# Attention with stacked rounded parts, values by tokens, two items a slot, and projections between the slots

## The reference

```
h  = norm0(x)*(1+scale)+shift
q,kc,vc,ks,vs,kw,vw,gl,z = h @ w_in           # NSA mixer
o  = g0*softmax(q k_cmp)v_cmp + g1*softmax(q ks)vs + g2*softmax(q kw)vw
x += gate_row0 * ((o * silu(z)) @ w_out)
# MoBA mixer: one causal softmax a head, 256 keys, the same form
x += gate_row1 * ((softmax(q k)v * silu(z)) @ w_out)
x += ffn1(norm(x)); x += mix(norm(x)) ; x += ffn2(norm(x))
```

## Time and profile before

| | us |
|---|---|
| median of 3 runs | 1009.32 (1008.92 to 1018.35) |
| the profiled execution, own time | 1017.86 |
| its span | 1016.0 |
| PE busy | 941.6 (93%) |
| DVE, ACT, POOL busy | 601.0, 515.5, 173.2 |

### The profile page before, as it was taken

One profiled execution on the slowest core, in us unless ns is written; L12 is line 12 of the kernel. 1 busy time (PEld: TensorE's weight loads), 2 busy tenths in 40 slices (PEclk: granted clock), 3 DMA queues, 4 the chain that ended last, 5 costly groups with the idle time before them and its releaser, 6 DMA issues.

```text
span 1016.0 us, 13211 instructions
## 1 busy us (share of the span) xinstructions
PE 941.6 (93%) x4823; PEld 763.2 (75%) x4823; DVE 601.0 (59%) x1192; ACT 515.5 (51%) x940; POOL 173.2 (17%) x190
## 2 busy tenths in 40 slices
PE   2689988998989988999999998999899899999997
PEld 2578976555568964788888887889788788888886
DVE  4873567766457577675555444659345765555542
ACT  2233556765434476564444443667555464444431
POOL 0015424652002651010000000426000200000000
PEclk9889999767699998999999999999999999999999
DMA  9855725444055453356555653645233555565651
GB/s 344 307 153 179 248 75 178 144 145 125 0 166 165 147 172 98 107 175 201 181 181 177 208 171 110 197 145 157 77 120 105 166 166 186 185 201 174 201 152 41
DMA packets 45391, 163.28 MB, mean 161 GB/s; under 512 B 5136, under 2 KB 5392, under 8 KB 45328
## 3 DMA queue, kind: packets, MB, share of 16 engines
q1 hardware_dynamic: 45328, 162.44, 50.0%
HBM read 161.37 MB, written 1.05 MB: 160 GB/s over the span
## 4 chain that ended last, share of the span: by engine, by line
PE 85%; DVE 8%; ACT 3%; issue 2%; DMA 1%; SPq 0%; POOL 0%; DVEq 0%; ACTq 0%
PE bank L451 55%; PE bank L460 11%; PE bank L475 5%; PE bank L610 3%; PE bank L589 2%; PE bank L588 2%; PE bank L504 2%; PE bank L547 1%; PE bank L612 1%; DVE w_lo L1313 1%; DVE ada_acc L1408 1%; PE bank L609 1%; DMA w_raw<-in_weights 1%; DVE stats L1494 1%; ACT soft L1007 1%
## 5 line engine op out<-in xcount | busy, mean ns | idle before, releaser
L888 ACT ACTIVATE w_hi<-w_raw 128x1024 fp32r<-128x1024 f32 (+2 forms) x249 | 259.2, 1047 | 203.0 <-PE bank L451 174.5
L1313 DVE TENSOR_TENSOR w_lo<-w_raw,w_hi 128x1024 fp32r<-128x1024 f32 (+2 forms) x249 | 300.8, 1224 | 101.3 <-ACT w_hi L888 101.3
L451 PE MATMUL bank<-w_hi,h_hi 128*128 128x512 f32 (+1 forms) x576 | 229.4, 398 | 15.6 <-DVE w_lo L1313 8.2
L451 PE MATMUL bank<-w_hi,h_lo 128*128 128x512 f32 (+1 forms) x576 | 225.4, 391 | 0.0
L451 PE MATMUL bank<-w_lo,h_hi 128*128 128x512 f32 (+1 forms) x576 | 224.9, 390 | 0.0
L451 PEld LDWEIGHTS bank<-w_hi,h_hi 128*128 128x128 f32 x576 | 109.5, 190 | 37.4 <-issue 16.5
L451 PEld LDWEIGHTS bank<-w_hi,h_lo 128*128 128x128 f32 x576 | 109.2, 190 | 22.9
L451 PEld LDWEIGHTS bank<-w_lo,h_hi 128*128 128x128 f32 x576 | 109.7, 190 | 20.9
L1952 POOL TENSOR_TENSOR ada_acc<-ada_acc,w_raw 128x512 f32<-128x512 f32 x56 | 73.4, 1311 | 84.0 <-ACT w_raw L892 79.4
L460 PE MATMUL bank<-h_hi,w_hi 128*128 128x256 f32 x264 | 77.9, 295 | 0.2 <-ACT tok_k L892 0.2
L460 PE MATMUL bank<-h_lo,w_hi 128*128 128x256 f32 x264 | 75.2, 285 | 0.0
(11 more groups left out here) (258 smaller groups left out, 1412.6 us busy)
## 6 DMA issues: line engine op xcount, KB each, us to landing
w_raw<-in_weights SPq DMA_DIRECT2D x298, 512.0 KB, 4.0
w_raw<-in_weights SPq DMA_DIRECT2D x4, 360.0 KB, 3.1
x<-in_x SPq DMA_DIRECT2D x1, 1024.0 KB, 7.0
gate_bias<-in_gate_bias SPq DMA_DIRECT2D x2, 512.0 KB, 9.4
out<-x SPq DMA_DIRECT2D x1, 1024.0 KB, 4.0
w_raw<-in_weights SPq DMA_DIRECT2D x3, 256.0 KB, 2.7
const<-in_constants SPq DMA_DIRECT2D x1, 413.5 KB, 7.7
cols<-in_columns SPq DMA_DIRECT2D x1, 208.5 KB, 2.5
```

Of the source, the lines that this page charges most:

```text
L451: mm = e.matmul(pb[t][:, 0:n], xs[q], ws[p], start=(k + kk == 0 and i == 0), stop=(k + kk == kts - 1 and i == 2))
L888: e.activation(w_hi[i % NSPLIT][:, 0:c], raw[v % NRAW][:, 0:c], ACT.Copy).then_inc(*rounded(v))
L1313: e.tensor_tensor(w_lo[i % NSPLIT][:, 0:c], raw[v % NRAW][:, 0:c], w_hi[i % NSPLIT][:, 0:c].bitcast(F32), ALU.subtract).then_inc(*rested(v))
```

## The change: what it does

- The two attentions are written anew (`pair_attention` on each engine). A slot is one head with both branches in NSA (16 slots) and two heads in MoBA (8). Queries are kept as `qs`, rounded part and rest stacked on 128 partitions; keys as `kh` and `kl`, each twice over the partitions. A score is two fp32r matmuls with K = 128 (kh, then kl), for both branches in one. Values are made by tokens: the turned probability is stationary, 65 columns move (64 of v and a column of ones that gives the sums). Compressed values go to the same bank (banks[7]). `evict` on DVE forms the factors (1/sum, gate) and multiplies 3 x 64 columns for both token tiles, adds the three, and stores by tokens; PE turns each closed pair of heads.
- The units of z1 come in iterations 0 to 3 of the NSA loop and six of out's eight in iterations 8 to 18, two after it. In MoBA z1 comes at 0 to 2 and five of out's eight at 6 to 10. The unit order follows.
- Ada chunks 4 and 5 of layer 0 (8 units, the gate row) are fetched among the units of q0, cmp0, q1 and cmp1, one after each two.
- Queries and keys are copied out in parts of 64 partitions: 8 copies of q (4 before), 8 of k of twice the width, and DVE subtracts the rests.
- The norm ahead of the mix turns x plainly, half of it inside the last feed-forward projection, half behind mix_lat's first unit. 1/rms is multiplied in later, at each use: eight DVE products of 512 for the gates, one more matmul of 256 columns, scales in copies for the rest.
- The bias of the gate row is loaded into gate_row itself. The output is stored in four DMAs of 256 KB.

The diff, cut to what matters:

```diff
+    z1, a, b, gate = one("nsa_z1"), ada(1, 0, 4), ada(1, 4, 6), ada(0, 4, 6)
+    heads = one("nsa_q0") + one("cmp_w1_0", CJ, 256, False) + one("nsa_q1") + one("cmp_w1_1", CJ, 256, False)
+    heads = [u for i in range(8) for u in heads[2 * i:2 * i + 2] + gate[i:i + 1]]
+    pair = lambda o, j: [o[j], o[4 + j]]
+    nsa = (in_turn(z1, a[:4]) + a[4:7] + pair(nsa_out, 0) + a[7:11] + pair(nsa_out, 1) + a[11:15]
+           + pair(nsa_out, 2) + a[15:] + pair(nsa_out, 3))
+    moba = (in_turn(b[:3], z[Z_FIRST:]) + b[3:5] + pair(moba_out, 0) + b[5:7] + pair(moba_out, 1) + b[7:]
+            + moba_out[2:4] + moba_out[6:8])
...
-             + kcvc[2:] + kskw[2:] + one("nsa_q0") + one("cmp_w1_0", CJ, 256, False)
-             + one("nsa_q1") + one("cmp_w1_1", CJ, 256, False) + one("nsa_gate", KT, P)
-             + one("nsa_vsvw") + one("nsa_z0") + in_turn(ada(0, 4, 6) + ada(1, 0, 4), one("nsa_z1"))
-             + two("nsa_out")
-             + two("moba_q") + one("moba_kv") + z[:Z_FIRST] + in_turn(ada(1, 4, 6), z[Z_FIRST:]) + two("moba_out")
+             + kcvc[2:] + kskw[2:] + heads + one("nsa_gate", KT, P)
+             + one("nsa_vsvw") + one("nsa_z0") + nsa
+             + two("moba_q") + one("moba_kv") + z[:Z_FIRST] + moba
...
+                def values(j):
+                    sl, x, p = slots[j // 2], j % 2, prob_t[j % 2]
+                    o = [ov[:, t, x + parts_ - 2, 0:HD + 1] for t in range(TT)]
+                    w.wait_ge(*p_copied.at((s, j)))
+                    for at in v_ready:
+                        w.wait_ge(*at)
+                    if x == 0:
+                        w.wait_ge(*(o_evicted.at((s, j // 2 - 1)) if j else bank_free[3]))
+                    e.matmul(o[0], p[:, 0:P], sl["values"][x][0], start=True, stop=True)
+                    e.matmul(o[1], p[:, P:2 * P], sl["values"][x][0], start=True, stop=False)
+                    mm = e.matmul(o[1], p[:, 2 * P:3 * P], sl["values"][x][1], start=False, stop=True)
+                    if x == 1 and sl["compressed"]:
+                        g, r = sl["compressed"]
+                        for t in range(TT):
+                            mm = e.matmul(ov[:, t, 0, 0:HD], pc_t[:, r, t * P:(t + 1) * P], vc[:, g, :], start=True,
+                                          stop=True)
+                    mm.then_inc(*valued((s, j)))
...
+                    if i < n:
+                        for t in range(TT):
+                            w.wait_ge(*(masked.at((s, i - 1, t)) if i else bank_free[t]))
+                            for o, q, ks in slots[i]["scores"][t]:
+                                for m, k in enumerate(ks):
+                                    mm = e.matmul(o, q, k, start=m == 0, stop=m == 1)
+                            mm.then_inc(*scored((s, i, t)))
+                    pr = slots[i - 4]["close"] if i >= 4 else None
+                    if pr is not None:
+                        w.wait_ge(*(o_summed if s == "nsa" else o_evicted).at((s, i - 4)))
+                        w.wait_ge(*p_copied.at((s, min(2 * (i - 3) + 1, 2 * n - 1))))
+                        turn(banks[6], [(tt * P, otok[:, tt, pr * P:(pr + 1) * P])
+                                        for tt in range(TT)]).then_inc(*o_turned((s, pr)))
+                        turned = pr
+                    if 0 <= i - 3 < n:
+                        values(2 * (i - 3) + 1)
+                    for x in range(2 if 0 <= i - 2 < n else 0):
+                        j = 2 * (i - 2) + x
+                        w.wait_ge(*exped.at((s, j, 1)))
+                        w.wait_ge(*(p_copied.at((s, j - 1)) if j else bank_free[2]))
...
+                        m = soft6[j % 6]
+                        turn(banks[6], [(c * P, m[:, c * P:(c + 1) * P]) for c in range(3)]).then_inc(*p_turned((s, j)))
+                        if x == 0:
+                            hook(i, 1)
+                        else:
+                            values(j - 1)
+                    if not 0 <= i - 2 < n:
+                        hook(i, 1)
...
+            outs = [linear("nsa_out0", 1, (o_hi, o_lo), o_of("nsa"), True, [z_done.at(("nsa_z1", 1))]),
+                    linear("nsa_out1", 0, (o_hi, o_lo), o_of("nsa"), True, [ada_cols.at(6), ada_cols.at(7)])]
...
+                if step == 0 and i in (1, 2):
+                    compressed_turns(i - 1)
+                if step == 1 and i < 4:
+                    next(z1)
+                if step == 1 and i in (8, 10, 12, 14, 16, 18):
+                    next(outs[i % 4 // 2])
+                if step == 1 and i in (5, 9):
+                    ada_columns(6 + i // 9, banks[i // 9], z_done.at(("nsa_z0", 1)))
...
+            ada_columns(8, banks[4], masked.at(("nsa", 15, 0)))
+            next(outs[0])
+            ada_columns(9, banks[5], masked.at(("nsa", 15, 1)))
+            next(outs[1])
...
+            def q_places(name, gain, p2, bank):
+                h = int(name[-1]) * 8 + 4 * p2
+                w.wait_ge(*cols_in.at())
+                w.wait_ge(*heads_turned.at((name, p2)))
+                for i, here in enumerate(HALVES):
+                    copy(qs[here, h:h + 4, :].rearrange("p (k i) s -> p i k s", i=2)[:, i, :, :],
+                         bank[here, :].rearrange("p (k s) -> p k s", k=2),
+                         scale=col(gain)[here, :]).then_inc(*heads_rounded((name, p2, i)))
+            def k_places(name, gain, br, bank):
+                w.wait_ge(*heads_turned.at((name, br)))
+                for i, here in enumerate(HALVES):
+                    for there in HALVES:
+                        copy(kh[there, :, br, :].rearrange("p (k i) s -> p i k s", i=2)[:, i, :, :],
+                             bank[here, :].rearrange("p (k s) -> p k s", k=2),
+                             scale=col(gain)[here, :]).then_inc(*heads_rounded((name, br, i)))
...
+                def evict(i):
+                    hs, h = slots[i]["heads"], slots[i]["heads"][0]
+                    w.wait_ge(*valued.at((s, 2 * i + 1)))
+                    if slots is nsa_slots:
+                        f = factors[:, :, :, h:h + 1]
+                        g = gates[:, :, :].rearrange("p t (b h) -> p t b h", b=3)[:, :, 1:3, h:h + 1]
+                        step(e.reciprocal(f[:, :, 1:3, :], ov[:, :, 1:3, HD:HD + 1]))
+                        stepped()
+                        step(e.tensor_tensor(f[:, :, 1:3, :], f[:, :, 1:3, :], g, ALU.mult))
+                        stepped()
+                        if i:
+                            w.wait_ge(*o_summed.at((s, i - 1)))
+                        e.tensor_tensor(parts_of_o[:, :, :, :], ov[:, :, :, 0:HD], bcast(f, [P, TT, 3, HD]),
+                                        ALU.mult).then_inc(*o_evicted((s, i)))
+                        w.wait_ge(*o_evicted.at((s, i)))
+                        e.reduce_sum(otok[:, :, h * HD:(h + 1) * HD],
+                                     parts_of_o[:, :, :, :].rearrange("p t b d -> p t d b"),
+                                     AX.X).then_inc(*o_summed((s, i)))
...
+                    if pr is not None:
+                        w.wait_ge(*o_turned.at((s, pr)))
+                        if pr > 1:
+                            w.wait_ge(*o_rested.at((s, pr - 2)))
+                        e.scalar_tensor_tensor(v[:, 0:S], banks[6][:, 0:S], 0.5, zs[:, pr, :], ALU.mult,
+                                               ALU.mult).then_inc(*o_gated((s, pr)))
+                    if i < n:
+                        maxima(i, 1)
+                    if 0 <= i - 3 < n:
+                        evict(i - 3)
+                    if pr is not None:
+                        w.wait_ge(*o_rounded.at((s, pr)))
+                        e.tensor_tensor(o_lo[:, pr, :], v[:, 0:S], o_hi[:, pr, :].bitcast(F32),
+                                        ALU.subtract).then_inc(*o_rested((s, pr)))
+                    hook(i, 1)
...
             head_power("nsa_kskw")
+            sum_chunk(4, 0)
             head_ropes("nsa_kskw", 0)
+            sum_chunk(4, 1)
             head_power("nsa_q0")
             head_ropes("nsa_kskw", 1)
+            sum_chunk(4, 2)
             power(kc_rs, kc_ms, kc_power(), kc_squared.at())
             head_ropes("nsa_q0", 0)
             rope(kc2[:, 0:1, 0:16], table(cs1, TT), table(sn1, TT), 1, 16, hn_roped, "kc", kc_normed.at())
             e.tensor_copy(kc2[:, 1, :], kc2[:, 0, :]).then_inc(*kc_doubled())
+            sum_chunk(4, 3)
             head_power("nsa_q1")
             head_ropes("nsa_q0", 1)
+            sum_chunk(5, 0)
+            sum_chunk(5, 1)
             head_ropes("nsa_q1")
-            for c in range(4, 10):
+            sum_chunk(5, 2)
+            sum_chunk(5, 3)
+            for c in range(6, 10):
                 for j in range(4):
                     sum_chunk(c, j)
...
-            e.dma_start(gate_bias[:, :], gate_bias_d[0:1, :].to_broadcast([P, D])).then_inc(*bias0_in())
-            for u in range(NRAW, of["moba_q0"][0]):
```

(19 more changed lines are left out.)

626 lines of the change are left out of this document (367 added, 259 removed).

## The result

The changed kernel takes 1049.13 us in the median (1048.60 to 1052.54, four runs) against 1013.32 for the kernel before (1008.92 to 1018.35). The ratio is 1.035, with a 95% interval of 1.030 to 1.040: slower by 36 us, where I had forecast 997, and outside the range. The profiled execution took 1048.84, its span is 1047.0. The kernel before scatters more than the changed one: of the 17 executions taken beside e5 to e8, six took 1004 to 1006 us and ten 1015 to 1018, and the profiled one (1017.86) is like the ten.

A forecast was written before the change was run, and what follows sets the result against it. PE was taken as the bound, busy 942 of 1016 us. Terms 19 − 27.5 − 1 − 6 − 1.3 = −17 gave 1001 from 1017.86; 4 off for a slow profiled execution gave 997, range 974 to 1016.

The forecast's parts named there:

- c: Second attention: five out units fill 9.1 idle us, against a later start and the slots' waits; −1 us, bounds −6 to +5.
- b: First attention: 32 items become 16 slots with less work and less time at 1.2 GHz; −27.5 us.
- a: Projections of q0 and q1: fetches wait for POOL's additions of gate units, so PE idles; +19 us, bounds 0 to +28.
- d: Norm before the mix: plain turns replace 32 f32 matmuls, 1/rms multiplied in later; −6 us.
- e: Output store: four stores of 256 KB instead of one of 1 MB; −1.3 us, bounds −1.3 to +1.
- +2 for work at 1.2 GHz: Front: cost of the slower clock after the idle stretches, on top of +17 of waits; +2 us.
- with a unit, 7.1: First attention: a slot holding an out unit takes 4.4 + 2.75 = 7.1 us, one without 5.0.
- as before 3.9: End of the first attention: the norm's DVE, ACT and POOL steps take an unchanged 3.9 us.
- D: Rival, attention loop: many small groups ended by waits keep PE at 1.2 GHz; +40 us, 1037; chance 0.14.
- E: Rival, attention slots: DVE's evictions meet POOL's additions and the next values wait; +14 us, 1011; chance 0.13.
- B: Rival, front: POOL's sums come early enough, fetches stay ahead and the front costs about 0; 980; chance 0.13.
- C: Rival, loops: PE stays at 2.4 GHz, so the slow-clock costs fall away; 984 us; chance 0.13.

The follow-up runs named there:

- e5: Changed kernel, MoBA only: ACT rounds the gated pair ahead of the two ada scalings, DVE subtracts its rest one slot later; 1034.14 us.
- e8: Kernel before the change, with only the new norm ahead of the mix and the four-part store; 1008.81 us against 1016.19, ratio 0.997.
- e2: Changed kernel with the gate row's eight units fetched later, one behind each unit of the projections vsvw and z0; 1026.93 us.
- e12: e9 with ACT's eight copies of the keys moved behind the roundings of the second compression's stretch; 987.07 us, 0.974 of the kernel before.
- e3: Changed kernel with rounding and subtraction of the out units in both attention loops done earlier, one unit an iteration; 1029.05 us.
- e1: Changed kernel with all of MoBA's out units moved behind its loop; 1048.06 us.
- e11: e9 with all of NSA's out units moved behind its loop; 1023.09 us.
- e9: e6 with DVE subtracting the keys' rests behind the scaling of q1's heads instead of ahead of it; 991.33 us.
- e6: Changed kernel with e2, e3 for NSA alone, e5, and squares of q1's heads ahead of the keys' copies; 991.44 us, 0.981 of the kernel before.
- e10: e9 with all of MoBA's out units moved behind its loop; 1002.55 us.

## Why the prediction was wrong

Between the two profiled executions I forecast −17 us and measured +31. Of these 48 us, 29.5 lie in MoBA (terms c), 11 in the first attention (b) and 8 in front (a); norm and store (d, e) are right to 1 us. The step that decided it is c: the claim that five units fill the idle time of a loop whose chain I hadn't walked. The 4 us that I took off because the profiled execution of the kernel before was a slow one don't appear either: the changed kernel's profiled execution is at its median (1048.84 and 1049.13).

- **Front (+19 forecast, +26.9).** Waits right in place and nearly in size: three of 13.4 us in sum, 15.5 forecast, and 16.4 us more of idle time in the whole stage, 17 forecast. (The eight copies of the keys were priced at 0.6 there and at 0.69 in c; they took 0.69.) The mis-sized step is the "+2 for work at 1.2 GHz": it ran 25 us more at that clock, 16 of them busy, which cost 8. The other 2.4 are busy time at the full clock. e2 takes the fetches' part away (17 us). Of the other 10, 6 are the keys' eight copies, which I had put only into the power of q1's heads: e12 takes them away by moving the copies behind the roundings in ACT's queue. 3.3 us stay unexplained.
- **First attention (−27.5 forecast, −16.1).** My sum with its extras and without the norm gives 134.9; the stage takes 147.8, and with the subtractions in time (e3) 125.9. So the slots themselves were priced 9 us too high: in e3 two slots with one unit take 10.7 to 11.2 us, where I had 12.1. The step that failed is the slot "with a unit, 7.1": I priced the unit as PE's work alone and did not ask when its subtraction on DVE would be done. It was late three times (9.0 us), and the clock fell behind it: 50 us at 1.2 GHz where I had 18. That is 22 us in e3's measure, and the 9 us too many hid part of it, which is luck. (The 96 matmuls of out in the sum for before come to 22.1, not 22.6; it changes nothing.) A smaller one is the norm "as before 3.9": PE's gap there is 7.6 us in the changed kernel, since both halves of out now end together and all four sums in x come behind the last unit.
- **MoBA's projections (+5.1; I had 3.3 of it, in c).** Right in kind, a little small: the copies and rests of keys and queries by 64 partitions delay the first score, behind a gap of 5.9 us.
- **Second attention (−1 forecast, +23.4): the step that decided it.** I wrote that five units "fill the 9.1 idle us". That counts idle time as room. In the changed kernel PE is idle for 23.1 us in this stage, where it was 7.8, and loses 15 us more to the clock. What stands in the place of my step is a chain that carries over from slot to slot: turns of the pair and of the probabilities share one bank, gating stands on DVE behind the previous pair's rest, that rest waits for ACT behind two scalings, and the units' subtractions come ahead of the gating as well. PE's turns wait 15.0 us for the gating. They wait 4.7 without the units (e1), 18.6 with the units' subtractions spread over more slots (e3), and 3.2 with scalings and rest out of the chain (e5). Only e5 keeps the units and with them the clock, and there 16.1 us of the stage go. The 87.0 are still 7 more than before: 7 us more of idle time and 6 for the clock, against 5 less of work. In that idle time are 5.3 us (four times) in which the last units wait for the pairs' rests; why the others stay isn't settled.
- **Norm (−6, measured −6.0) and store (−1.3, measured −2.1)**: right, and e8 shows the norm's in the kernel before. The store's term compared landing times, 2.7 and 4.0; what counts is the end behind the last sum, 5.2 and 3.1 us, and three of the four parts are issued before that sum is done.
- **The rivals.** D (1.2 GHz through the loop, 1037) had the right sign and a part of the cause: 91 us of the two attentions ran at 1.2 GHz, 79 of them busy, and before it was 72 and 69. So against the kernel before the clock costs 5 us more there and 8 in front, not 40; against my forecast, which had 18 us at 1.2 GHz in the first attention and none more in the second, it is 28. What I had against D, units of long matmuls in every second iteration, is right as e11 shows, and was annulled by the waits: e3 takes most of them away in the first attention, and its clock is 0.92. The Trainium skill, "TensorE: Matmul & The Clock Gate", section "A second HAM failure mode: psum-queue depth-cycling", says that PE idling briefly between groups of matmuls, often enough, makes the clock swing. e11 agrees with it (0.72 with 20.8 us idle in many short waits), but e9 has 19.5 us idle and 0.93, so idle time alone doesn't decide it. E (evictions wait for POOL) has its mechanism in the trace and not its price: the product of factors and gates (L1619), 0.17 us by itself, ran into an addition of POOL six times in 16 and then ended with it, after 0.29 to 0.96 us, but values wait for an eviction 0.7 us in all in the changed kernel. B and C would have needed no gaps in front and a clock above 0.9; neither was so.

No rival had the loop-carried chain in MoBA, though the diff shows it: the wait on o_gated ahead of the turns, and the rest ahead of the hook on DVE.

## What to carry to other kernels

Before you count idle time as room for work, walk one iteration's chain through every queue, and put the new work's own preparation (rounding, subtraction) into the queues where it stands: it must be done an iteration ahead, behind nothing that waits, and ahead of nothing that PE waits for (e3 helped one loop and not the other). A wait taken off PE was worth 1.4 to 2.2 times its length here, since the clock came back with it: 11.9 us of idle time gave 17.0 in e2, 9.8 gave 21.9 in e3, 8.4 gave 16.1 in e5. Another order of nearly the same instructions (e12) made a change that cost 3.5% into one that gains 2.6%.

## What the runs showed of the hardware

- Units of twelve 512-column matmuls between the slots kept the clock up, at nearly the same idle time: the first attention has 0.93 with six units inside and 0.72 without (e9, e11), the second 0.80 and 0.73 in the changed kernel (e1), 0.93 and 0.87 with the cures (e6, e10). It is no rule for other loops: the second attention before the change has 0.96 with no such unit inside.
- A small operation of DVE that meets an addition of POOL (128x512) can last as long as that addition: the product of 128x4 values took 0.95 us and ended at 234.01, POOL's addition at 233.99; by itself it takes 0.17.
- Where work at 1.2 GHz falls is not fixed by a stage's own program: in e8 the old attentions took 154.2 and 90.3 us instead of 163.9 and 79.7, after a front that was 0.8 us longer. Whether that shift is the reason isn't shown.
- Fp32r scores with 256 and 512 moving columns against a 128-column weight cost nearly what the projections' do: four in 0.76 us, 0.69 forecast from them. Three float32 value matmuls of 65 columns, six passes, take 0.61 us, 0.66 forecast. A copy of 512 elements on 64 partitions takes 0.68 us, no less than on 128 (0.69 in the earlier trace rows).
